# The rolled attention histories of a hybrid decoder step: DRAM copies moved from the latent decode into the first three MLPs

## What is computed

```
for i in range(DEPTH):
    sh1, sc1, g1, sh2, sc2, g2 = adaln(c, ada_w[i], ada_b[i])
    x = x + g1 * mixer_i(modulate(x, norm1_g[i], sh1, sc1))
    x = x + g2 * (square(relu(modulate(x, norm2_g[i], sh2, sc2) @ w1)) @ w2)
```

```
keep = min(w, lb + s)
states.append(jnp.stack([kf[:, lb + s - keep:], vf[:, lb + s - keep:]], axis=2))
```

## Time and profile before

| | before |
|---|---|
| median of 3 runs | 2712.25 us (2711.92 to 2725.25) |
| the profiled execution: its time | 2710.68 us |
| the profiled execution: span from first to last instruction | 2708.5 us |
| mean granted TensorE clock | 0.876 |
| busy: PE, DVE, ACT, POOL | 2372.6, 1086.3, 834.3, 26.9 us |
| DMA queue of SP (q1): MB, share of 16 engines over the span | 332.69 MB, 37.6% |
| DMA queue of POOL (q0) | 59.76 MB, 6.6% |
| MLPs 0, 1, 2, 3, from their first matmul | 266.6, 1185.2, 1506.4, 2470.6 us |
| latent decode, from its first scores to the last weighted sums | 1964.0 to 2402 us |

### The profile page before, as it was taken

One profiled execution on the slowest core, in us unless ns is written; L12 is line 12 of the kernel. 1 busy time (PEld: TensorE's weight loads), 2 busy tenths in 40 slices (PEclk: granted clock), 3 DMA queues, 4 the chain that ended last, 5 costly groups with the idle time before them and its releaser, 6 DMA issues.

```text
span 2708.5 us, 34137 instructions
## 1 busy us (share of the span) xinstructions
PE 2372.6 (88%) x13554; PEld 1985.0 (73%) x13554; DVE 1086.3 (40%) x1730; ACT 834.3 (31%) x1469; POOL 26.9 (1%) x54
## 2 busy tenths in 40 slices
PE   4697999999789999889997899988897667788998
PEld 1495988899678677578885788863586556667998
DVE  0353552377231011155436553357633223325642
ACT  0322442254221111144322442243332222314532
POOL 0000000000100000000000000000000000000000
PEclk8798999999775656699998999998698888889999
DMA  7542676533323333147762477534005533333542
GB/s 296 219 142 93 204 256 229 166 109 117 109 68 108 105 105 105 35 140 257 256 214 79 160 259 249 179 101 156 19 18 176 166 134 119 119 125 102 153 152 86
DMA packets 229347, 398.70 MB, mean 147 GB/s; under 512 B 9272, under 2 KB 195423, under 8 KB 215649
## 3 DMA queue, kind: packets, MB, share of 16 engines
q1 hardware_dynamic: 224912, 332.69, 37.6%
q0 software_dynamic: 3296, 59.76, 6.6%
q10 hardware_dynamic: 1017, 4.48, 0.4%
HBM read 391.37 MB, written 59.76 MB: 167 GB/s over the span
## 4 chain that ended last, share of the span: by engine, by line
PE 77%; DVE 9%; DMA 8%; ACT 2%; issue 2%; SPq 2%; ACTq 0%; POOL 0%; DVEq 0%; POOLq 0%
PE bank L982 33%; PE bank L912 10%; PE bank L1389 5%; PE bank L1187 5%; PE bank L874 4%; PE bank L1162 4%; DMA work<-in_cache_mla 4%; PE bank L956 3%; DVE rstd L1539 2%; PE bank L1074 2%; PE bank L927 2%; DMA ring<-in_ada_w 2%; PE bank L1398 1%; DVE hT L1454 1%; DMA ring<-in_mlp_w 1%
## 5 line engine op out<-in xcount | busy, mean ns | idle before, releaser
L1475 DVE TENSOR_TENSOR ring_lo<-ring,ring_hi 128x1024 fp32r<-128x1024 f32 (+1 forms) x324 | 379.0, 1213 | 424.5 <-ACT ring_hi L593 424.5
L593 ACT ACTIVATE ring_hi<-ring 128x1024 fp32r<-128x1024 f32 (+1 forms) x324 | 322.8, 1046 | 462.8 <-PE bank L982 183.3
L982 PE MATMUL bank<-h_hi,ring_hi 128*128 128x320 f32 x1024 | 326.5, 319 | 27.6 <-DVE h_lo L1450 27.3
L982 PE MATMUL bank<-hidden_hi,ring_hi 128*128 128x320 f32 x1024 | 322.2, 315 | 0.0
L982 PE MATMUL bank<-h_lo,ring_hi 128*128 128x320 f32 x1024 | 320.3, 313 | 0.0
L982 PE MATMUL bank<-h_hi,ring_lo 128*128 128x320 f32 x1024 | 319.6, 312 | 0.0
L982 PE MATMUL bank<-hidden_hi,ring_lo 128*128 128x320 f32 x1024 | 318.3, 311 | 0.0
L982 PE MATMUL bank<-hidden_lo,ring_hi 128*128 128x320 f32 x1024 | 318.1, 311 | 0.0
L874 PE MATMUL bank<-tab,work 128*128 128x128 f32 (+6 forms) x708 | 159.0, 373 | 174.8 <-DMA work<-in_cache_mla 85.9
L874 PEld LDWEIGHTS bank<-tab,work 128*128 128x128 f32 (+6 forms) x708 | 107.3, 185 | 209.3 <-issue 99.5
L982 PEld LDWEIGHTS bank<-h_hi,ring_hi 128*128 128x128 f32 x1024 | 196.3, 192 | 63.1 <-issue 60.7
(11 more groups left out here) (232 smaller groups left out, 3361.7 us busy)
## 6 DMA issues: line engine op xcount, KB each, us to landing
ring<-in_mlp_w SPq DMA_DIRECT2D x128, 1024.0 KB, 7.4
work<-in_ada_w SPq DMA_DIRECT2D x72, 1024.0 KB, 5.0
ring<-in_ada_w SPq DMA_DIRECT2D x24, 1024.0 KB, 8.8
work<-in_state_swa SPq DMA_DIRECT2D x80, 256.0 KB, 7.1
ring<-in_swa_w_qkv SPq DMA_DIRECT2D x18, 1024.0 KB, 5.0
work<-in_state_swa SPq DMA_DIRECT2D x16, 1024.0 KB, 6.2
out_swa_s<-in_state_swa POOLq DMA_DIRECT2D x8, 2016.0 KB, 10.0
ring<-in_conv_w_in SPq DMA_DIRECT2D x12, 1024.0 KB, 5.1
```

Source lines behind the costliest of these rows:

```text
L593: act.activation(ring_hi[:, place, part], ring[:, s, part], ACT.Copy).then_inc(sem("weights_hi"), 1)
L982: mm = pe.matmul(bank[a % 4][:, 0:T], w[:, k, :], x(k), start=first and k == 0 and j == 0, stop=last and k == KD - 1 and j == 2)
L1475: dve.tensor_tensor(ring_lo[:, s, part], ring[:, s, part], ring_hi[:, place, part], ALU.subtract)\
```

## The change

The copies of the eight sequences leave their loop at the end of POOL's list. A function `roll(n, phase, units)` waits until the first `units` units of a phase are done and then issues the three copies of sequence n. Copies 0, 1 and 2 are issued in the first MLP (after its unit 0, its unit 8 and its unit 17), 3, 4 and 5 at the same places of the second, 6 and 7 in the third, after its unit 0 and unit 8. The lists of SP, PE, ACT and DVE keep their instructions and their order; only line numbers shift.

```diff
--- before.py
+++ after.py
@@ -491,11 +491,24 @@
         def _(gp):
             gp.memset(vec_in[0:64, 2, :], 0.0).then_inc(sem("vec_cleared"), 1)
             store(gp, O["pool_s"][0, :, 0:HIST - SS], A["state_pool"][0, :, SS:HIST])
+
+            def roll(n, phase, units):
+
+                gp.wait_ge(sem("unit_done"), UNIT0[phase] + units)
+                for g in range(G):
+                    rows = SWA_KEEP[g]
+                    lost = SWA_KEEP[g] + SS - O[f"swa{g}_s"].shape[2]
+                    store(gp, O[f"swa{g}_s"][0, n, 0:rows - lost].rearrange("l k h d -> l (k h d)"),
+                          A[f"state_swa{g}"][0, n, lost:rows].rearrange("l k h d -> l (k h d)"))
+
             gp.wait_ge(sem("conv_state_out"), 2)
             gp.dma_start(O["conv_p"].rearrange("a b r d -> (a b r) d"), cv_out[0:2, :]).then_inc(sem("conv_rows_stored"), 16)
             gp.dma_start(O["conv_s"].rearrange("a n r d -> (a n r) d"), cv_out[2:18, :]).then_inc(sem("conv_rows_stored"), 16)
 
 
+            roll(0, "mlp1_0", 1)
+            roll(1, "mlp1_0", 9)
+            roll(2, "mlp2_0", 2)
             wait_banks(gp, "swa_out")
             for i, (g, t) in enumerate(KEY_TILES):
                 gp.wait_ge(sem("key_tile_copied"), i + 1)
@@ -517,22 +530,19 @@
                 gp.dma_start(O[f"swa{g}_s"][0, :, r0:r0 + SS, 1].rearrange("n s h d -> n s (h d)"), v[0:TS, 2, :])\
                   .then_inc(sem("values_stored"), 16)
 
+            roll(3, "mlp1_1", 1)
+            roll(4, "mlp1_1", 9)
+            roll(5, "mlp2_1", 2)
             gp.wait_ge(sem("pool_state_out"), 4)
             gp.dma_start(O["pool_p"].rearrange("a b r d -> (a b r) d"), pl_out[P - HIST:P, 0, :]).then_inc(sem("pool_rows_stored"), 16)
             gp.dma_start(O["pool_s"][0, :, HIST - SS:HIST], pl_out[0:TS, 1, :]).then_inc(sem("pool_rows_stored"), 16)
 
+            roll(6, "mlp1_2", 1)
+            roll(7, "mlp1_2", 9)
             gp.wait_ge(sem("latent_tok"), 3)
             gp.dma_start(O["mla_p"].rearrange("a b (t p) e -> p (a b t) e", p=P), ml_tok[:, 0:2, :]).then_inc(sem("latent_rows_stored"), 16)
             gp.dma_start(O["mla_s"].rearrange("a n s e -> (a n s) e"), ml_tok[0:TS, 2, :]).then_inc(sem("latent_rows_stored"), 16)
 
-            for n in range(NS):
-                if n:
-                    gp.wait_ge(sem("md_pv"), n)
-                for g in range(G):
-                    rows = SWA_KEEP[g]
-                    lost = SWA_KEEP[g] + SS - O[f"swa{g}_s"].shape[2]
-                    store(gp, O[f"swa{g}_s"][0, n, 0:rows - lost].rearrange("l k h d -> l (k h d)"),
-                          A[f"state_swa{g}"][0, n, lost:rows].rearrange("l k h d -> l (k h d)"))
 
             gp.wait_ge(sem("y_copied"), 6)
             store(gp, O["y_prompt"].rearrange("a (t p) d -> p (a t) d", p=P), y_out[:, 0:2, :])
```

## The result

The changed kernel takes 2745.27 us (median of 6 runs, 2739.12 to 2746.41) against 2712.53 us for the kernel before on the same chip: a ratio of 1.0103, 95% interval 1.0080 to 1.0127. It is slower, by 33 us; 2730 was forecast, with 2688 to 2755 as the range.

A forecast was written before the change was run, and what follows sets the result against it. TensorE was taken to bound the kernel (77% of the chain of waits, DMA 8%). From 2710.68 us, a gain of 82 us and a cost of 101 us gave 2730 us, range 2688 to 2755.

The forecast's parts named there:

- The gain: Latent decode: copies 1 to 6 no longer meet page loads, saving 13.65 us each, 82 us (78 to 86).
- two hand-overs: Latent decode, between sequences: scores' end to next weighted sums takes 26.1 us with pages there, 39.8 us with pages late.
- the one microsecond of spare: Latent decode: last page load would land at 2041.9, TensorE asks at 2042.98, so pages are in time by one microsecond.
- The hold: MLPs: a load issued with a copy lands 22.8 us after the copy's start, plus engine time of loads queued up to it.
- Case A: Copies 1, 4, 7, 2, 5 in the MLPs' steady part: loads for unit 11 late, 15.8 us each, 79 us for five.
- Case B: Copies 0, 3, 6 behind unit 0 of an MLP: load of unit 4 late, 7.5 us each, 22 us for three.
- The idles: First three MLPs: eight new TensorE idles, five of 13.8 us and three of 6.1 us.
- The cost: First three MLPs: weight loads held by eight copies, idle and clock loss together 101 us (72 to 125).
- the clock: MLPs: TensorE's clock falls in an idle, adding 2 us in the steady part and 1.4 us behind unit 0.
- Rival 1: MLPs: loads and copies share the DMA engines evenly, so loads land sooner; faster, 2652 us; chance 0.17.
- Rival 2: MLPs: load of unit 4 mostly passes before the second copy packet, early copies free; no change, 2708 us; chance 0.20.
- Rival 3: MLPs: loads have not caught up before the next copy, or the clock stays at half longer; 2750 us; chance 0.08.

The follow-up runs named there:

- experiment 5: Changed kernel, copies at the same places but rows cut to 3.75 to 4 KB instead of 30 to 64 KB: 2724.49 us.
- experiment 6: Changed kernel, copies at the same places but rows cut to about 1 KB: 2720.11 us.
- experiment 9: Changed kernel, copies at the same places but rows of 2048 and 4096 bytes, for copy packets of 4096 bytes: 2688.98 us.
- experiment 4: Against a kernel with all copies where no weights load (2631.45 us), copies 1, 2, 4, 5, 7 put back in the MLPs: 2714.72 us.
- experiment 3: Against a kernel with all copies where no weights load (2631.45 us), copies 0, 3, 6 put back behind unit 0 of the MLPs: 2660.78 us.

## Why the prediction was right

**The gain.** Forecast 13.65 us for each of six meetings, 82 us; measured 81.8 us. The reading of two hand-overs was exact, VectorE's wait included. The pages land 2.2 us after their issue, so the one microsecond of spare was enough.

**The hold.** Forecast: a load issued with a copy lands 22.8 us after it, plus the engine time of what is queued up to it. Case A: forecast 28.95 us after the unit's end, measured 348.13 + 27.78 = 375.9, with the end at 346.7, 29.2 us. There the weight load did come behind the copy, whose last data packet ended at 371.4; the conditioning block ahead of it passed during the copy and not behind it, and the copy lasted longer than the forecast had it (24.4 us from its issue). Case B: forecast 25.9, measured 301.8 - 274.8 = 27.0. Here the number is near, but the way to it was another: the forecast put the load's 3.1 us behind a hold of 22.8. In the run nine tenths of the load passed ahead of the copy, nothing of its 3.1 us was left to come behind, and the hold alone was 26.7 us from the copy's issue (275.06), since the copy's packets began only at 279.4 and the load's last seven packets on an engine were drawn out to its end. That the two errors nearly cancel is luck.

Experiments 5, 6 and 9 show the cause that was only read from the earlier trace rows: the engine gives each queue one packet in turn. A load lasts as many turns as it has packets left, or, where the copy has fewer packets than that, until the copy is over. The reading of the earlier trace rows was a little off in its counts: 16 of the 144 and 16 of the 96 packets are of 4 bytes, so it was eight load packets an engine in the first gap, and 89 load packets beside 80 copy packets of 64 KB. One for one stands.

**The idles.** Case A forecast 13.8 us, measured 12.9 to 14.3, mean 13.4. Case B forecast 6.1, measured 7.4, 6.7 and 8.2, mean 7.4.

**What was mis-sized.** The cost was forecast at 101 us and is 112 to 115. Two terms fell short: the clock, put at 2 and 1.4 us, is some 3.3 us in case A and 2.4 in case B (16.7 and 9.8 us in experiments 4 and 3, less the idles); and the idle of case B by 1.3 us. At copy 1 a product runs in the midst of the idle at half speed (1.93 us where 1.0 is usual), and the 48 matmuls behind it take 9.93 us where 7.23 is usual: 0.9 and 2.7 us. The net forecast of 19 us slower came out at 33, at the upper end of what the forecast's own mechanism was given (2715 to 2745).

**The rivals.** Rival 1, even sharing, had 2652 us. The Trainium skill ("DMA: Bandwidth & Descriptors", Queues, rings and completion order) has whole packets of 9 to 17 descriptors drained in a turn. Here a load row of 1 KB or 8 KB passed as a packet of its own against copy packets of 4 to 64 KB (552 beside 552, 510 beside 510, 103 beside 104). On the other side the same section's rule, that an engine takes the queues in turn packet by packet, is just what the traces show, with "packet" as the profile counts it. Rival 2, free early copies, falls by experiment 3, and its own condition makes it worth a second look: most of the load did pass before the second copy packet, and it cost 7.4 us of idle all the same. Rival 3 had two branches with 2750 us. That loads pile up falls by the sum of 3 and 4; that the clock costs more than was put down is part of why the time came out 15 us above the forecast. That the nine load packets in the first gap of the decode spoke for rival 1 is a misreading to avoid: they passed between the copy's first and second packet, which the later alternation does not explain, and I can only suppose that the copy's queue stood empty there.

## What to carry to other kernels

A background copy from DRAM to DRAM is not free because the DMA engines have time left: while it runs, each load packet waits for one copy packet, so a load of many 1 KB rows is held for nearly the whole copy, even if all but seven of its packets on an engine have passed before. Put such copies where nothing is loaded, or let them wait for the landing of the loads that they would meet, or give them out in pieces no longer than the loads' slack. Before moving work to where a resource looks half idle, compare the slack of one load there (6 us here) with the length of the thing that will hold it (22 us), not with the share of the span.

## What was unexpected of the hardware

SP's own issue can block. Just before TensorE stalls at copy 1, SP's timeline has 12.66 us on one issue that takes 0.34 us elsewhere, with one pair of loads outstanding behind the copy:

```profile
355.98 12.66 SPq L390 DMA_DIRECT2D work<-in_ada_w  x1
368.68 2.91 SPq L376 DMA_DIRECT2D ring<-in_mlp_w  x1
```

No further idle of TensorE follows from it here; whether a full queue is the cause was not tried. Also new to me: POOL's transfers join short rows into packets of 4096 bytes or more, where SP's loads keep 1 KB rows apart (992 load packets of 1024 bytes and 128 of 8192 in the 18 us shown of run 9), and that the queues go one for one, 552 and 552.
